# Query and key row transposes issued behind the next projection row block instead of ahead of it

## The chip, the cores and the metric

The kernel runs on one core of a Trainium2 chip. The metric is the device time of one execution in microseconds, of which the median of three runs is given.

## What is computed

One layer of a hybrid decoder for 1024 prompt tokens and 32 sample tokens. One projection `u = RMSNorm(x) @ w_in` gives the columns of three branches (a state-space scan, a dilated attention and a cross-attention), which are merged by gates. The change lies in the attention branch's part of that projection:

```
qkv = qkv.reshape(b, t, ATT_N_GROUPS, 3, ATT_HEADS, ATT_HEAD_DIM)
q = _rope(qkv[:, :, :, 0], pos)
k = _rope(qkv[:, :, :, 1], pos)
v = qkv[:, :, :, 2]
for gi in range(ATT_N_GROUPS):                 # (window, dilation) = (128,1), (512,4), (2048,16)
    o, l = _dilated_prompt(q[:, :, gi], k[:, :, gi], v[:, :, gi], w, d)
```

`_rope` turns the first 16 of each head's 64 columns by an angle that depends on the token. `_dilated_prompt` is a windowed softmax attention in blocks of 128 queries.

## The kernel before

`plan()` writes out one list of steps, `sched`. Every engine walks that list in the same order and issues its own part of each step, so the list fixes the order of work on each engine, and semaphores between engines do the rest. Engines issue in order: an instruction that waits holds back all that stands behind it on its engine.

The attention projection goes by three groups `g` and two halves `h` (four heads, 256 columns each). For each (g, h) there are three chunks of weights, q, k and v, and each chunk has nine row steps `("tok", n, t)`: eight blocks of 128 prompt tokens and one of the sample tokens (t = 8). A row step is on TensorE 24 matmuls of 128x256 (L2287 to L2289, three products of split operands over eight k tiles; for t = 8 of q, k and v 16 matmuls, L2385 and L2386) into one of three PSUM banks. ScalarE evicts it into one of four slots of `rows` (L1515, "eviction" below), VectorE rotates the row there in four instructions (L1820 to L1823, "rotation"; the last one signals `s_rope`). Then the step `("turn", n, t)` transposes the rotated block: two TensorE transposes into bank 3 (L2419), and VectorE copies bank 3 to `QT` or `KT` (L1841, "copy", signals `s_turned`).

`heads_steps` puts these steps in a row. A turn waits in a list, and one is taken out at a row step once three are in it. `around` and `spread` then lay the attention units of the half computed before among the row steps. A unit has the groups: its `scores` (L2441, into banks 3 and 4) with the `ptrans` of the unit before (probabilities transposed, L2458), its `softmax` (no TensorE work), and the `pv` of the unit before (L2483). Each of the five blocks of row steps from (g, h) = (0, 1) to (2, 1) has the eight units 0 to 7 of the half before among its 27 row steps.

Bank 3 is shared by turns and scores, so each waits for the reader of the other:

```
elif s[0] == "turn":                                   # TensorE
    pe.wait_ge(s_rope, roped[("tok", n, t)] + 1)
    if scored_before[s]:
        pe.wait_ge(s_msk3, scored_before[s])           # scores' bank 3 read (DVE L1897)
    if v >= 1:
        pe.wait_ge(s_turned, v)                        # the turn before copied out
elif s[0] == "scores":
    pe.wait_ge(s_turned, max(turns_before[s], ...))    # all turns before it copied out
```

VectorE reads the scores with L1897 ("mask", two instructions; the first signals `s_msk3`). It also makes `w_lo` of coming weights, a step `("low", n)` of one long instruction (L1753). At its end `plan()` puts each of these behind a `pv`, and behind the turn that follows it if one follows directly. Permuting the normalised tokens (`perm`) stands ahead of block (1, 0).

Of the kernel before, what the change touches and what calls it, by code (L numbers as in the profile page):

```python
# [119 lines left out]
def plan():  # L120
# [7 lines left out]
    def chunk(kind, detail, src, col):  # L128
        chunks.append((kind, detail, src, col))
        return len(chunks) - 1  # L130
# [40 lines left out]
    def heads_steps(qkv):  # L171

        steps, waiting = [], []
        for n in qkv:
            kind = chunks[n][0]
            for t in range(NB + 1):
                now = [waiting.pop(0)] if len(waiting) >= 3 or (kind == "v" and waiting) else []
                steps.append(now + [("tok", n, t)])
                if kind != "v" and t < NB:
                    waiting.append(("turn", n, t))  # L180
            steps.append([("split", n)])
        return steps
# [53 lines left out]
    for g in range(NG):  # L236
        for h in range(2):
            qkv = [chunk(k, (g, h), "w_in", C_QKV + g * 3 * AW + j * AW + CW * h) for j, k in enumerate("qkv")]
            if h == 0 and g in PASS_AT:
                sched.insert(len(sched) - 1, ("perm", PASS_AT[g]))  # L240
            sched += around(todo, heads_steps(qkv))
            todo = [unit("att", g, b, h) for b in range(NB)]
# [20 lines left out]
    def gate_steps(k):  # L263

        steps = []
        for n in take(k):
            for s in project(n) + [("split", n)]:
                if s[0] in ("split", "silu"):
                    steps[-1].append(s)
                else:  # L270
                    steps.append([s])
        return steps
# [16 lines left out]
    steps = gate_steps(round(total))  # L289
# [6 lines left out]
    steps = gate_steps(1) + [[]]  # L296
# [22 lines left out]
    steps = []  # L319
    for i in range(4):  # L320
        n = chunk("p1", 2 * i, "att+mem", CW * i)
# [9 lines left out]
    for i in range(4):  # L331
        n = chunk("p2", 2 * i, "w_br_ssd", CW * i)
        sched += [("p2", n, f, j) for f in range(2) for j in range(3)] + [("split", n)]
    for i in range(4):
        n = chunk("out", i, "w_out", CW * i)
# [2445 lines left out]
```

## Time and profile before

| | us |
|---|---|
| median of three runs (lowest, highest) | 2127.19 (2124.83, 2128.45) |
| the profiled execution, its own time | 2122.49 |
| its span in the trace | 2120.6 |
| TensorE matmul busy | 1978.7 (93%) |
| VectorE busy | 984.6 (46%) |
| ScalarE busy | 763.9 (36%) |
| GpSimd busy | 241.5 (11%) |

The profile is of one execution. Its time is the number against which a sum of durations is made; the median of the three runs is what a comparison is made with. The busy share of TensorE counts its matmuls with modelled ends, so what a step costs there is read from the starts of matmuls.

### The profile page before, as it was taken

The page shows a single profiled execution, that of the slowest core. Times are in us where ns is not written, and L with a number is a line of the kernel's source. Part 1 is how long each engine was busy: PE and PEld are TensorE (multiplying, and loading weights), DVE is VectorE, ACT ScalarE, POOL GpSimd, SP SyncE. Part 2 cuts the span into 40 slices and gives each one's busy share as a digit, 9 for nine tenths or more (in the row PEclk, how much of TensorE's full clock was granted, in tenths as well). Part 3 has the DMA queues.
Part 4 walks back from the last instruction along what each step waited for, and adds up shares of the span by engine and source line. Part 5 has one row for each costly group of instructions (what it writes and reads, how often), then busy time and mean ns, then how long its engine had stood idle before and what let it go on. Part 6 is the DMA issues. An engine that isn't in the chain of part 4 may idle for free.

```text
span 2120.6 us, 34809 instructions
## 1 busy us (share of the span) xinstructions
PE 1978.7 (93%) x14301; PEld 1887.0 (89%) x14301; DVE 984.6 (46%) x1941; ACT 763.9 (36%) x1642; POOL 241.5 (11%) x358
## 2 busy tenths in 40 slices
PE   5999999999979999999999899999999859969997
PEld 5899999999979999999999898769999759969997
DVE  5313676535465353534236676103454545454423
ACT  5223354223343333323555322215566532132202
POOL 1001111100001010111111200001121111100000
PEclk9999999999999999999999999999999869989999
DMA  6211332311101111122246675683455536454422
GB/s 216 90 42 52 93 92 82 93 46 48 40 30 51 54 49 57 61 64 83 68 147 220 224 255 163 228 281 124 150 160 176 202 102 191 166 181 137 144 83 105
DMA packets 171742, 257.18 MB, mean 121 GB/s; under 512 B 20229, under 2 KB 115269, under 8 KB 171557
## 3 DMA queue, kind: packets, MB, share of 16 engines
q1 hardware_dynamic: 149328, 187.97, 28.1%
q0 software_dynamic: 22256, 66.98, 9.3%
q8 instruction: 114, 1.87, 0.4%
q14 instruction: 44, 0.36, 0.1%
HBM read 188.13 MB, written 66.76 MB: 120 GB/s over the span
## 4 chain that ended last, share of the span: by engine, by line
PE 76%; DVE 8%; ACT 6%; DMA 5%; issue 3%; SPq 0%; DVEq 0%; POOL 0%; ACTq 0%; POOLq 0%
PE bank L2287 19%; PE bank L2288 19%; PE bank L2289 19%; PE bank L2483 2%; DVE w_lo L1753 2%; PE bank L2698 2%; PE bank L2458 2%; DMA acc<-acc_T 2%; PE bank L2441 1%; PE bank L2587 1%; PE bank L2419 1%; ACT soft L1579 1%; PE bank L2742 1%; PE bank L2520 1%; DMA sums<-sum_T 1%
## 5 line engine op out<-in xcount | busy, mean ns | idle before, releaser
L2287 PE MATMUL bank<-w_hi,hT_hi 128*128 128x256 f32 (+1 forms) x1848 | 535.7, 290 | 1.4 <-issue 1.4
L2288 PE MATMUL bank<-w_lo,hT_hi 128*128 128x256 f32 (+1 forms) x1848 | 523.8, 283 | 0.0
L2289 PE MATMUL bank<-w_hi,hT_lo 128*128 128x256 f32 (+1 forms) x1848 | 522.9, 283 | 0.0
L2287 PE MATMUL bank<-hT_hi,w_hi 128*128 128x352 f32 x1344 | 450.8, 335 | 6.3 <-DVE acc L2134 5.6
L2289 PE MATMUL bank<-hT_hi,w_lo 128*128 128x352 f32 x1344 | 438.9, 327 | 0.0
L2288 PE MATMUL bank<-hT_lo,w_hi 128*128 128x352 f32 x1344 | 438.2, 326 | 0.0
L2287 PEld LDWEIGHTS bank<-w_hi,hT_hi 128*128 128x128 f32 (+1 forms) x1848 | 348.7, 189 | 3.2 <-issue 1.6
L2289 PEld LDWEIGHTS bank<-w_hi,hT_lo 128*128 128x128 f32 (+1 forms) x1848 | 349.6, 189 | 0.6
L2288 PEld LDWEIGHTS bank<-w_lo,hT_hi 128*128 128x128 f32 (+1 forms) x1848 | 348.7, 189 | 1.3
L2287 PEld LDWEIGHTS bank<-hT_hi,w_hi 128*128 128x128 f32 x1344 | 257.7, 192 | 20.1 <-issue 8.4
L2288 PEld LDWEIGHTS bank<-hT_lo,w_hi 128*128 128x128 f32 x1344 | 258.5, 192 | 0.5
L2289 PEld LDWEIGHTS bank<-hT_hi,w_lo 128*128 128x128 f32 x1344 | 256.7, 191 | 0.0
L1753 DVE TENSOR_TENSOR w_lo<-w_raw,w_hi 128x2048 fp32r<-128x2048 f32 x64 | 146.4, 2287 | 199.6 <-ACT w_hi L1425 199.5
L1515 ACT ACTIVATE rows<-bank 128x256 f32<-128x256 f32 (+2 forms) x172 | 65.2, 379 | 329.5 <-PE bank L2289 285.5
L1425 ACT ACTIVATE w_hi<-w_raw 128x2048 fp32r<-128x2048 f32 x64 | 122.1, 1908 | 77.6 <-PE bank L2289 48.9
L1579 ACT ACTIVATE soft<-soft,nmax 128x256 f32<-128x256 f32 (+1 forms) x224 | 100.0, 448 | 80.2 <-DVE nmax L1917 79.9
L1549 ACT ACTIVATE fstage<-bank 128x256 f32<-128x256 f32 (+5 forms) x168 | 56.5, 459 | 142.6 <-PE bank L2289 142.4
L1820 DVE TENSOR_TENSOR small<-rows,con 128x32 f32<-128x32 f32 (+1 forms) x108 | 20.5, 190 | 187.6 <-ACT rows L1515 187.3
L1897 DVE TENSOR_TENSOR soft<-bank,con 128x256 f32<-128x256 f32 (+1 forms) x96 | 47.7, 537 | 51.3 <-PE bank L2441 51.2
L2483 PE MATMUL bank<-V,softT 128*128 128x64 f32 x560 | 67.7, 270 | 0.8 <-issue 0.8
L2483 PEld LDWEIGHTS bank<-V,softT 128*128 128x128 f32 x560 | 66.6, 192 | 1.0 <-issue 1.0
L1946 DVE COPY obuf<-bank 128x256 f32<-128x256 f32 x48 | 20.2, 421 | 99.3 <-PE bank L2483 99.3
(423 smaller groups left out, 2926.1 us busy)
## 6 DMA issues: line engine op xcount, KB each, us to landing
w_raw<-in_w_in SPq DMA_DIRECT2D x96, 512.0 KB, 5.0
kvring<-in_cache_win_kv SPq DMA_DIRECT2D x98, 256.0 KB, 4.7
feat_T<-fstage POOLq DMA_DIRECT2D x40, 528.0 KB, 4.0
fstage<-feat_T SPq DMA_DIRECT2D x16, 528.0 KB, 4.6
xc<-feat_T SPq DMA_DIRECT2D x8, 1024.0 KB, 5.8
sums<-sum_T SPq DMA_DIRECT2D x32, 256.0 KB, 4.5
o_rows<-obuf POOLq DMA_DIRECT2D x48, 132.0 KB, 2.0
mo<-o_rows SPq DMA_DIRECT2D x24, 264.0 KB, 3.6
```

The costliest lines, as they stand in the source:

```text
L1425: act.activation(w_hi[:, n % 2, :, :], w_raw[:, :, :], ACT.Copy).then_inc(s_whi, 1)
L1515: act.activation(dst, psum, func).then_inc(s_pjev, 1)
L1549: ins = act.activation(dst[:, to], psum[:, c0:c1], func)
L1579: ins = act.activation(soft[:, a % 2, h, 0:w], soft[:, a % 2, h, 0:w], ACT.Exp, bias=nmax[:, a % 2, h:h + 1], scale=scale, accum_out=total)
L1753: dve.tensor_tensor(w_lo[:, n % 2, :, :], w_raw[:, :, :], w_hi[:, n % 2, :, :].bitcast(F32), ALU.subtract).then_inc(s_wlo, 1)
L1897: ins = dve.tensor_tensor(dst, src, con[:, c0:c0 + w].unsqueeze(1).broadcast_to([P, 2, w]), ALU.add)
L2287: pe.matmul(out, xh(k), wh(k), start=(k == 0), stop=False)
L2288: pe.matmul(out, xh(k), wl(k), start=False, stop=False)
L2289: ins = pe.matmul(out, xl(k), wh(k), start=False, stop=(k == nk - 1))
L2458: ins = pe.transpose(bank[5 + h // 2][:, c0:c0 + P], soft[:, a % 2, h, P * k:P * k + P], ident)
L2483: ins = pe.matmul(bank[7][:, HD * h:HD * h + HD], softT[:, a % 2, h, k, :], V[:, b0 + k, c0:c0 + HD], start=(k == 0), stop=(k == kb - 1))
L2698: ins = pe.matmul(bank[5 if h < 8 else 7][0:m, SP * (h % 8):SP * (h % 8) + SP], Lm_of(c, h // 4)[:, h % 4, :], xdt[0:m, SP * h:SP * h + SP ...
```

## The change

```diff
@@ heads_steps
             for t in range(NB + 1):
                 now = [waiting.pop(0)] if len(waiting) >= 3 or (kind == "v" and waiting) else []
-                steps.append(now + [("tok", n, t)])
+                steps.append([("tok", n, t)] + now)
                 if kind != "v" and t < NB:
                     waiting.append(("turn", n, t))
```

Which turn is taken out at which row step stays as it was; it now stands behind that row step. So when it is issued, one more row has been projected. In the 96 places where a turn stood ahead of a row step the two swap. `spread` cuts its groups at the ends of row steps, so a turn that is now the last of its row step can stand directly ahead of the next group. No instruction is added or taken away, apart from where VectorE's `w_lo` stands: that step now comes directly behind its `pv` and no longer behind a turn.

**TensorE, block (0, 1), around the scores of unit 5.** Row-step matmuls are L2287 to L2289. Before:

```order
L2289 MATMUL bank<-w_hi,hT_lo 128x256
L2441 MATMUL bank<-KT,QT 128x256 x4
L2458 MATMUL bank<-con,soft 128x128 x8
L2419 MATMUL bank<-con,rows 128x128 x2
L2287 MATMUL bank<-w_hi,hT_hi 128x256
```

Now:

```order
L2289 MATMUL bank<-w_hi,hT_lo 128x256
L2419 MATMUL bank<-con,rows 128x128 x2
L2441 MATMUL bank<-KT,QT 128x256 x4
L2458 MATMUL bank<-con,soft 128x128 x8
L2287 MATMUL bank<-w_hi,hT_hi 128x256
```

The turn behind scores and transposed probabilities went behind the next row step, and another turn came in between the row step and the scores.

**VectorE at the same place**, from the rotation of the row ahead of the scores to the next row's. Before:

```order
L1820 TENSOR_TENSOR small<-rows,con 128x4x8
L1821 TENSOR_TENSOR small<-rows,con 128x4x8
L1822 TENSOR_TENSOR rows<-rows,con 128x4x16
L1823 TENSOR_TENSOR rows<-rows,small 128x4x16
L1897 TENSOR_TENSOR soft<-bank,con 128x2x256 x2
L1929 COPY softT<-bank 128x512
L1841 COPY KT<-bank 128x2x128
L1820 TENSOR_TENSOR small<-rows,con 128x4x8
```

Now:

```order
L1820 TENSOR_TENSOR small<-rows,con 128x4x8
L1821 TENSOR_TENSOR small<-rows,con 128x4x8
L1822 TENSOR_TENSOR rows<-rows,con 128x4x16
L1823 TENSOR_TENSOR rows<-rows,small 128x4x16
L1841 COPY KT<-bank 128x2x128
L1897 TENSOR_TENSOR soft<-bank,con 128x2x256 x2
L1929 COPY softT<-bank 128x512
L1820 TENSOR_TENSOR small<-rows,con 128x4x8
```

The copy of the turn ahead of the scores now stands directly behind the rotation of the newest row, and ahead of the mask.

**VectorE in block (0, 1), ahead of the scores of unit 2**, where `w_lo` (L1753) is made. Before:

```order
L1823 TENSOR_TENSOR rows<-rows,small 128x4x16
L1946 COPY obuf<-bank 128x256
L1841 COPY QT<-bank 128x2x128
L1753 TENSOR_TENSOR w_lo<-w_raw,w_hi 128x2048
L1820 TENSOR_TENSOR small<-rows,con 128x4x8
L1821 TENSOR_TENSOR small<-rows,con 128x4x8
L1822 TENSOR_TENSOR rows<-rows,con 128x4x16
L1823 TENSOR_TENSOR rows<-rows,small 128x4x16
L1897 TENSOR_TENSOR soft<-bank,con 128x2x256 x2
```

Now:

```order
L1823 TENSOR_TENSOR rows<-rows,small 128x4x16
L1841 COPY QT<-bank 128x2x128
L1946 COPY obuf<-bank 128x256
L1753 TENSOR_TENSOR w_lo<-w_raw,w_hi 128x2048
L1820 TENSOR_TENSOR small<-rows,con 128x4x8
L1821 TENSOR_TENSOR small<-rows,con 128x4x8
L1822 TENSOR_TENSOR rows<-rows,con 128x4x16
L1823 TENSOR_TENSOR rows<-rows,small 128x4x16
L1841 COPY QT<-bank 128x2x128
L1897 TENSOR_TENSOR soft<-bank,con 128x2x256 x2
```

The long instruction stays where it was against the output copy (L1946) and the rotation; a copy came in behind that rotation. ScalarE, GpSimd and the DMA queue of SyncE have the same instructions in the same order as before.

## Rows read from the trace of the kernel before

**Rows 1.** The page: TensorE's busy time, and its granted clock in 40 slices.
```profile
PE 1978.7 (93%) x14301; PEld 1887.0 (89%) x14301; DVE 984.6 (46%) x1941; ACT 763.9 (36%) x1642; POOL 241.5 (11%) x358
...
PEclk9999999999999999999999999999999869989999
```
**Rows 2.** Busy time by engine, sum of the five blocks' stretches (432 us).
```profile
sum 432.00, PE 414.01 PEld 394.25 DVE 225.64 ACT 136.95 POOL 41.40; mean PE 82.80 PEld 78.85 DVE 45.13 ACT 27.39 POOL 8.28
```
**Rows 3.** Waits of TensorE, 484 to 1000 us: total, times, longest.
```profile
PE bank L2419 <- DVE rows L1823: 12.1, 12, 2.0
```
**Rows 4.** TensorE in order of time (start, us, line), scores of unit 5.
```profile
538.71 0.28 PE L2289 MATMUL bank<-w_hi,hT_lo 128*128 128x256 f32 x1
538.92 1.13 PE L2441 MATMUL bank<-KT,QT 64*128 64x256 f32 x8
539.98 1.09 PE L2458 MATMUL bank<-con,soft 128*128 128x128 f32 x8
...
541.20 0.36 PE L2287 MATMUL bank<-w_hi,hT_hi 128*128 128x256 f32 x1
```
**Rows 5.** ScalarE and VectorE at the same place.
```profile
539.11 0.38 ACT L1515 ACTIVATE rows<-bank 128x256 f32<-128x256 f32 x1 [2.96 <-PE bank L2289]
...
540.11 0.22 DVE L1823 TENSOR_TENSOR rows<-rows,small 128x64 f32<-128x64 f32 x1
```
**Rows 6.** TensorE, unit 3 of the same block, where no turn follows.
```profile
512.45 0.28 PE L2386 MATMUL bank<-w_lo,hT_hi 128*64 128x256 f32 x1
...
514.56 0.36 PE L2287 MATMUL bank<-w_hi,hT_hi 128*128 128x256 f32 x1
```
**Rows 7.** TensorE and VectorE, unit 6 of block (1, 1).
```profile
781.38 0.28 PE L2386 MATMUL bank<-w_lo,hT_hi 128*64 128x256 f32 x1
782.40 0.72 PE L2441 MATMUL bank<-KT,QT 64*128 64x128 f32 x8 [0.74 <-DVE KT L1841]
...
784.11 0.36 PE L2287 MATMUL bank<-w_hi,hT_hi 128*128 128x256 f32 x1
...
781.84 0.41 DVE L1841 COPY KT<-bank 128x256 f32<-128x256 f32 x1
```
**Rows 8.** TensorE and VectorE, unit 2 of block (0, 1), behind `w_lo`.
```profile
499.14 0.28 PE L2289 MATMUL bank<-w_hi,hT_lo 128*128 128x256 f32 x1
...
502.77 0.36 PE L2287 MATMUL bank<-w_hi,hT_hi 128*128 128x256 f32 x1
...
501.68 0.22 DVE L1823 TENSOR_TENSOR rows<-rows,small 128x64 f32<-128x64 f32 x1
```
**Rows 9.** TensorE, unit 1 of block (1, 0), behind the permutation.
```profile
607.46 0.66 PE L2458 MATMUL bank<-con,soft 128*128 128x128 f32 x4 [2.11 <-ACT soft L1579]
610.13 0.66 PE L2419 MATMUL bank<-con,rows 128*128 128x128 f32 x2 [2.01 <-DVE rows L1823]
...
615.48 0.28 PE L2289 MATMUL bank<-w_hi,hT_lo 128*128 128x256 f32 x1
```
**Rows 10.** TensorE, unit 5 of block (2, 1), one key block per unit.
```profile
978.84 0.28 PE L2289 MATMUL bank<-w_hi,hT_lo 128*128 128x256 f32 x1
979.05 0.72 PE L2441 MATMUL bank<-KT,QT 64*128 64x128 f32 x8
...
981.07 0.37 PE L2287 MATMUL bank<-w_hi,hT_hi 128*128 128x256 f32 x1
```
**Rows 11.** TensorE, unit 1 of block (0, 1).
```profile
486.88 0.27 PE L2289 MATMUL bank<-w_hi,hT_lo 128*128 128x256 f32 x1
...
489.34 0.36 PE L2287 MATMUL bank<-w_hi,hT_hi 128*128 128x256 f32 x1
```
**Rows 12.** By stretch: busy us (count) of PE, PEld, DVE, ACT, POOL; granted clock; DMA.
```profile
608.60:615.40 6.80, 5.27 (x25) 5.30 (x26) 2.63 (x8) 0.00 (x0) 0.00 (x0) 0.50 0.01 4
615.50:1209.30 593.80, 574.13 (x4756) 553.66 (x4755) 278.43 (x728) 232.23 (x598) 84.97 (x154) 1.00 0.29 95
...
1272.60:1275.10 2.50, 0.04 (x1) 0.00 (x1) 2.50 (x3) 0.00 (x0) 0.00 (x0) 0.82 0.40 149
```

## The prediction

> **What bounds the kernel now.** I read the page first, then the five blocks alone, then the waits, then single places in order of time. TensorE is busy for 93% of the span at nearly full clock [rows 1], and for 414.0 of 432 us in the blocks that the change touches, with VectorE at 225.6 and ScalarE at 137.0 [rows 2]. So a microsecond by which TensorE starts its next row step later is a microsecond of the end, and work of the other engines is free unless TensorE waits for it. The waits show what the edit aims at: 12.1 us, 12 times, in which a turn waited for VectorE's rotation [rows 3]. The name is that of an instruction; the semaphore that was late is the mask's, which stands right behind the rotation.
>
> I measure each place by one number: from the start of the last row-step matmul ahead of the scores (T) to the start of the first matmul of the next row step. At unit 5 of block (0, 1) it is 541.20 - 538.71 = 2.49 us [rows 4]; at unit 3, where no turn follows the scores, 514.56 - 512.45 = 2.11 us [rows 6]. The difference, 0.38 us, is what the turn and its wait cost there.
>
> **What the change does at these places.** Each of the five blocks has eight units. Units 0 and 7 have no turn near. Unit 1 loses a turn behind its scores and gets none ahead. Unit 3 gets one ahead of its scores and had none behind. Units 2, 4, 5 and 6 have both: the one behind goes, another comes ahead. The remaining turns only swap with a row step or a `pv` and cost the same there. So 25 scores get a turn directly ahead (5 x 5), and 25 turns behind scores go (units 1, 2, 4, 5, 6).
>
> **The wait that comes.** Scores wait until every turn before them is copied out of bank 3. That copy now stands on VectorE behind the rotation of the newest row, and the rotation waits for the eviction of the very row step that TensorE has just finished. All of it is visible: with T = 538.71 the eviction starts at T + 0.40 and takes 0.38, and the rotation ends at 540.11 + 0.22, T + 1.62 [rows 5]. The copy takes 0.41 us and starts about 0.08 before the rotation's end, as neighbours on VectorE do here, so it ends at T + 1.95. Scores that waited for such a copy exist already: it ended at 781.84 + 0.41 = 782.25, the scores began at 782.40, 0.15 later [rows 7]. New start of the scores: T + 2.09, against T + 0.21 now [rows 4]. Each new wait costs **1.88 us**, the turn's own issue in it included. Nothing hides it, since scores, probabilities and the next row step stand behind it on TensorE.
>
> Nineteen of the 25 are of this kind: 19 x 1.88 = 35.7. In three of them (unit 4 of blocks (0, 1), (1, 0) and (2, 1)) the row is also evicted into a slot whose turn now stands behind it; I add 0.25 us each, about one transpose: 0.7.
>
> In the other six (unit 2 of the first four blocks, unit 4 of the third and fourth) the rotation stands behind `w_lo`. There it ends at 501.68 + 0.22 = 501.90, T + 2.76 [rows 8]. The edit takes a copy of 0.41 from ahead of `w_lo`, but puts one ahead of the previous row maximum, so the exponentials, the eviction behind them, the rotation and the output copy come 0.33 later: net 0.08 earlier. Scores start at T + 2.68 + 0.47 = T + 3.15, which is 2.94 later than now: 6 x 2.94 = 17.6. Together the new waits come to **54.0 us**.
>
> **The waits that go.** A turn behind the scores waited for the mask; now a whole row step is between, so it is covered.
> - Units 4, 5, 6 of the first two blocks: 0.38 at the place shown, 0.64 at unit 4. I take 0.45 x 6 = 2.7.
> - Units 5 and 6 of the next two: at 781.38 the place takes 2.73 [rows 7], of which 1.02 is a wait that stays as part of the new one, and scores and probabilities take the rest but for the turn. A place of this width without a turn, scores at T + 0.21, would take 1.70. So 1.03, at unit 5 about 0.8: 0.92 x 4 = 3.7.
> - Units 2, 4, 5, 6 of the last block: 981.07 - 978.84 = 2.23 [rows 10], and 1.27 without the turn. 0.96, a little more beside `w_lo`: 1.03 x 4 = 4.1.
> - The six behind `w_lo`: 502.77 - 499.14 = 3.63 [rows 8] against 2.11, so 1.52, and 1.65 at the four places of the narrower blocks: 2 x 1.52 + 4 x 1.65 = 9.6.
> - Unit 1: 489.34 - 486.88 = 2.46 [rows 11] against 1.68 (narrow probabilities), 0.78 three times, 0.95 in the last block: 3.3.
> - Unit 1 behind the permutation. The turn begins 2.67 us after the probabilities, and the row step behind it runs at half clock until 615.48 [rows 9, 12]. With the row step directly behind the probabilities it starts at about 607.9 and, if the half clock up to there is as now and ends one step of its length earlier, ends at about 612.2 instead of 615.5. I take 3.3.
>
> Removed in all: **26.7 us**. Everything outside the 40 places costs what it did: block (0, 0) has no units, and its turns and row steps swap freely; `w_lo` comes no later; no DMA moves, and their queues keep their order. What follows the blocks starts later by the same amount and waits for nothing new.
>
> **The sum.** 54.0 - 26.7 = +27.3 us on the profiled execution's 2122.5: 2149.8. The median of the runs lies 4.7 above that execution, so I expect 2127.2 + 27.3 = 2154.5 us, rounded up to **2155**. A new wait cannot be below 0.81 us, the one that exists at 781.38 (1.02 - 0.21), and I see none above the 2.94 behind `w_lo`. With these ends for all 25 the sum is 20.3 - 26.7 = -6.4 and 73.5 - 26.7 = +46.8. I stay with the middle because the chain behind it is in the rows link by link.
>
> **Rivals.**
> *The clock falls.* In the six places behind `w_lo` TensorE would stand idle for about 2.6 us between the turn and the scores, and about 1.5 us in the others. The granted clock was 1.00, its 2.4 GHz level, from 615.5 to 1209.3 us, and 0.50, 1.2 GHz, for 6.8 us from 608.6, around the waits of 2.1 and 2.0 us [rows 9]; it began to fall in a wait of 2.5 us at 1272.6 [rows 12]. A row step at half clock took 5.0 us (610.44 to 615.48) against 2.85. If each of the six places cost one such step, that is 6 x 2.2 = 13 us more: 2168. If all 25 did, 2210, but dense row steps stand on both sides of every wait, and eleven of the twelve waits of [rows 3] lie where the clock stayed at 1.00. The Trainium skill, "TensorE: Matmul & The Clock Gate", section "A second HAM failure mode", says that frequent short idle times between groups of matmuls make the throttle come and go, with a warm-up to pay each time. By that rule the trace agrees only for the stretch at 605 to 615.
>
> *The new wait is short, and the kernel is faster.* If VectorE had the copy done before the rotation of the new row, as at 781.84, where the copy belongs to an earlier turn, each new wait would be 0.81 us and the time 2127.2 - 6.4 = 2121. It decides at 26.7 / 25 = 1.07 us per new wait. Against it: the order on VectorE puts rotation ahead of copy at all 25 places, and the rotation alone ends 1.62 us behind T.
>
> *The waits only trade places.* If both kinds were alike, 25 go and 25 come, and nothing is measured: 2127. The mask's wait is hidden in part by the scores and probabilities (1.9 us of TensorE work), the copy's by nothing, which is why I give it little.
>
> **How the numbers follow.** Forecast 0.74, clock 0.19, shorter wait 0.04, trade 0.03. About 0.2% (4.3 us) is what a measurement of this kernel can tell from no change. The range goes from 2146 (each wait 0.35 us shorter) to 2167 (the clock case for nearly all of the six). Faster 0.04, same 0.03, slower 0.93.
>
> **What would show it.** In the changed kernel's profile: scores (L2441) waiting for VectorE's copies (L1841) about 25 times, some 1.5 us each and 2.6 in six, together near 45 us; the turn's waits (L2419) nearly gone; the places of 2.49 and 2.11 us both at about 4.0; the permutation's place shorter by about 3. It would be wrong if scores begin less than 1.5 us behind T, if turns still wait, or if the granted clock is below 1.00 in the blocks from 620 us on.

## The result and the profile after

| | before | changed |
|---|---|---|
| median of the runs, us | 2126.38 (4 runs, 2124.83 to 2128.45) | 2167.94 (4 runs, 2163.98 to 2170.81) |
| ratio to before, 95% interval | | 1.020 (1.0184 to 1.0216) |
| profiled execution, us | 2122.49 | 2163.98 |
| its span | 2120.6 | 2162.2 |
| from the first to the last attention scores matmul | 598.9 | 643.8 |

The change costs 41.6 us. The forecast was 27.3 (2155, range to 2167): the sign and the new waits held, the size did not, and the result lies just outside the range.

TensorE's waits between 484 and 1060 us in the changed kernel, by what was waited for: us in total, times, longest.

```profile
PE bank L2441 <- DVE QT L1841: 33.7, 15, 3.1
PE bank L2441 <- DVE KT L1841: 14.6, 10, 1.6
PE bank L2313 <- ACT hT_hi L1562: 4.5, 3, 3.3
PE bank L2458 <- ACT soft L1579: 2.1, 1, 2.1
PE bank L2419 <- DVE KT L1841: 1.5, 2, 0.8
```

The scores (L2441) wait for the copy of a turn 25 times, 48.3 us together; the 12.1 us of turns that waited for a rotation [rows 3] are gone. The forecast said 25 times and about 45 us.

The place of [rows 4] and [rows 5], scores of unit 5 in block (0, 1), in the changed kernel. TensorE, ScalarE, VectorE in order of time:

```profile
544.44 0.28 PE L2289 MATMUL bank<-w_hi,hT_lo 128*128 128x256 f32 x1
544.56 0.38 PE L2419 MATMUL bank<-con,rows 128*128 128x128 f32 x2
546.55 1.13 PE L2441 MATMUL bank<-KT,QT 64*128 64x256 f32 x8 [1.61 <-DVE KT L1841]
```
```profile
544.84 0.38 ACT L1515 ACTIVATE rows<-bank 128x256 f32<-128x256 f32 x1 [2.69 <-PE bank L2289]
```
```profile
545.26 0.19 DVE L1820 TENSOR_TENSOR small<-rows,con 128x32 f32<-128x32 f32 x1 [1.59 <-ACT rows L1515]
...
545.84 0.23 DVE L1823 TENSOR_TENSOR rows<-rows,small 128x64 f32<-128x64 f32 x1
545.99 0.42 DVE L1841 COPY KT<-bank 128x256 f32<-128x256 f32 x1
```

With T = 544.44, the start of the last row-step matmul, the eviction begins at T + 0.40, the rotation ends at T + 1.63, the copy at T + 1.97, the scores begin at T + 2.11. The prediction had T + 0.40, 1.62, 1.95 and 2.09.

At unit 2 of block (1, 1), behind `w_lo`, the same chain is longer, and something else comes with it. TensorE, then VectorE:

```profile
746.46 0.28 PE L2289 MATMUL bank<-w_hi,hT_lo 128*128 128x256 f32 x1
746.58 0.38 PE L2419 MATMUL bank<-con,rows 128*128 128x128 f32 x2
749.99 1.23 PE L2441 MATMUL bank<-KT,QT 64*128 64x128 f32 x8 [3.03 <-DVE QT L1841]
...
753.34 0.41 PE L2289 MATMUL bank<-w_hi,hT_lo 128*128 128x256 f32 x1
753.55 0.41 PE L2287 MATMUL bank<-w_hi,hT_hi 128*128 128x256 f32 x1
```
```profile
745.84 0.41 DVE L1841 COPY QT<-bank 128x256 f32<-128x256 f32 x1
746.18 0.41 DVE L1946 COPY obuf<-bank 128x256 f32<-128x256 f32 x1
746.51 2.28 DVE L1753 TENSOR_TENSOR w_lo<-w_raw,w_hi 128x2048 fp32r<-128x2048 f32 x1
748.71 0.18 DVE L1820 TENSOR_TENSOR small<-rows,con 128x32 f32<-128x32 f32 x1
...
749.43 0.42 DVE L1841 COPY QT<-bank 128x256 f32<-128x256 f32 x1
```

The wait is 3.03 us, and the row step behind it issues a matmul every 0.21 us instead of every 0.12. Busy times by stretch (PE, PEld, DVE, ACT, POOL, then the granted clock) show seven such stretches outside the permutation's:

```profile
629.80:636.40 6.60, 6.08 (x27) 5.34 (x28) 2.36 (x5) 0.60 (x1) 0.00 (x0) 0.50 0.52 161
530.80:534.10 3.30, 3.30 (x18) 2.65 (x15) 1.70 (x3) 0.41 (x1) 0.00 (x0) 0.50 0.82 285
749.30:756.00 6.70, 6.01 (x31) 5.82 (x32) 1.99 (x5) 0.60 (x1) 0.00 (x0) 0.50 0.51 159
780.00:786.70 6.70, 6.16 (x32) 5.96 (x33) 1.84 (x5) 0.60 (x1) 0.00 (x0) 0.50 0.52 157
810.70:814.00 3.30, 3.30 (x20) 3.08 (x18) 1.45 (x3) 0.60 (x1) 0.00 (x0) 0.50 0.15 43
899.50:902.80 3.30, 3.30 (x18) 3.30 (x17) 0.69 (x1) 0.60 (x1) 0.00 (x0) 0.50 0.66 234
926.80:930.10 3.30, 3.30 (x20) 3.08 (x19) 1.27 (x3) 0.52 (x1) 0.07 (x1) 0.50 0.20 57
```

In all of them the clock is at 1.2 GHz, half its upper level, and TensorE is nearly always busy, so this is work done slowly and no wait. Before the change the clock was 1.00 from 615.5 to 1209.3 us [rows 12]. These 33 us are the candidate for what the sum lacked; the experiments had to tell them from longer waits. Below, a "fall" is the beginning of such a stretch at half clock.

### The profile page after: what moved, and what is told of

Same layout as the page of the kernel before. It is cut to its first block, busy times and chain, and to the rows that moved or that the text cites. A ratio compares the mean times of both kernels' runs of the same rounds, so it can differ in the third digit from the quotient of the medians.

```text
span 2162.2 us, 34809 instructions
## 1 busy us (share of the span) xinstructions
PE 1984.2 (92%) x14301; PEld 1895.2 (88%) x14301; DVE 988.4 (46%) x1941; ACT 765.1 (35%) x1642; POOL 241.4 (11%) x358
## 4 chain that ended last, share of the span: by engine, by line
PE 75%; DVE 9%; ACT 6%; DMA 6%; issue 3%; SPq 0%; DVEq 0%; ACTq 0%; POOL 0%; POOLq 0%
PE bank L2287 18%; PE bank L2288 18%; PE bank L2289 18%; PE bank L2458 2%; PE bank L2483 2%; PE bank L2441 2%; DVE w_lo L1753 2%; DMA acc<-acc_T 2%; PE bank L2698 2%; PE bank L2587 1%; ACT soft L1579 1%; DMA sums<-sum_T 1%; PE bank L2742 1%; PE bank L2520 1%; PE bank L2386 1%
## 5 line engine op out<-in xcount | busy, mean ns | idle before, releaser
L2287 PE MATMUL bank<-w_hi,hT_hi 128*128 128x256 f32 (+1 forms) x1848 | 538.1, 291 | 1.4 <-DVE hT_lo L2157 1.4
L2289 PE MATMUL bank<-w_hi,hT_lo 128*128 128x256 f32 (+1 forms) x1848 | 524.6, 284 | 0.0
L2287 PE MATMUL bank<-hT_hi,w_hi 128*128 128x352 f32 x1344 | 448.7, 334 | 6.2 <-DVE acc L2134 5.6
L2289 PE MATMUL bank<-hT_hi,w_lo 128*128 128x352 f32 x1344 | 437.1, 325 | 0.0
L2287 PEld LDWEIGHTS bank<-w_hi,hT_hi 128*128 128x128 f32 (+1 forms) x1848 | 351.4, 190 | 3.2 <-issue 1.7
L2289 PEld LDWEIGHTS bank<-w_hi,hT_lo 128*128 128x128 f32 (+1 forms) x1848 | 351.8, 190 | 0.6
L2287 PEld LDWEIGHTS bank<-hT_hi,w_hi 128*128 128x128 f32 x1344 | 256.0, 190 | 19.9 <-issue 8.4
L2289 PEld LDWEIGHTS bank<-hT_hi,w_lo 128*128 128x128 f32 x1344 | 255.5, 190 | 0.0
L1753 DVE TENSOR_TENSOR w_lo<-w_raw,w_hi 128x2048 fp32r<-128x2048 f32 x64 | 146.4, 2287 | 197.3 <-ACT w_hi L1425 197.3
L2441 PE MATMUL bank<-KT,QT 64*128 64x128 f32 (+1 forms) x384 | 46.6, 363 | 48.4 <-DVE QT L1841 33.7
L2441 PEld LDWEIGHTS bank<-KT,QT 64*128 64x128 f32 x384 | 32.0, 198 | 57.3 <-issue 54.7
```

The lines of the kernel that those rows point to most:

```text
L1753: dve.tensor_tensor(w_lo[:, n % 2, :, :], w_raw[:, :, :], w_hi[:, n % 2, :, :].bitcast(F32), ALU.subtract).then_inc(s_wlo, 1)
L2287: pe.matmul(out, xh(k), wh(k), start=(k == 0), stop=False)
L2289: ins = pe.matmul(out, xl(k), wh(k), start=False, stop=(k == nk - 1))
L2441: ins = pe.matmul(bank[3 + h % 2][:, CW * (h // 2):CW * (h // 2) + kb * P], QT[r:r + 64, i, P * b:P * b + P], KTt[r:r + 64, i, P * b0:P * ...
```

## The experiments

Nine kernels ran. "Blocks" is the time from the first to the last attention scores matmul of the profiled execution, which leaves out what varies ahead of and behind the blocks. It is 598.9 us before and 643.8 after. Each ratio is to executions of the kernel before that were taken beside the run; their medians are 2125.6 us (e1 to e4), 2125.9 (e5 to e7) and 2124.7 (e8, e9). Line numbers shift with an edit: the scores (L2441) are L2445 in e1 and e3, L2448 in e2 and L2452 in e5, the turns (L2419) L2423 in e7 and L2426 in e4, the copies (L1841) L1845, L1848 or L1852.

| | what differs | us, median | ratio to before (95%) | blocks, us |
|---|---|---|---|---|
| changed | | 2167.9 | 1.020 (1.0184 to 1.0216) | 643.8 |
| e1 | copy ahead of the rotation | 2130.1 | 1.0028 (1.0014 to 1.0042) | 610.2 |
| e2 | waits filled with transposes | 2161.5 | 1.0167 (1.014 to 1.0195) | 629.8 |
| e3 | `w_lo` behind the scores | 2149.6 | 1.0107 (1.0087 to 1.0128) | 621.5 |
| e4 | turn ahead of the row step before scores | 2168.5 | 1.0199 (1.018 to 1.0218) | 646.1 |
| e5 | e4 and e1 | 2104.6 | 0.990 (0.9883 to 0.9916) | 579.1 |
| e6 | e1 and e3 | 2118.3 | 0.997 (0.9959 to 0.9982) | 594.0 |
| e7 | kernel before with `w_lo` behind the scores | 2120.4 | 0.9978 (0.9967 to 0.9988) | 595.3 |
| e8 | filled behind `w_lo` only | 2154.3 | 1.0145 (1.0127 to 1.0162) | 632.2 |
| e9 | filled elsewhere only | 2166.5 | 1.0203 (1.0188 to 1.0218) | 641.8 |

**e1, the copy ahead of the rotation.** Edit of the changed kernel, VectorE alone:

```diff
-            for s in sched:
+            dve_sched = list(sched)
+            for i in range(len(sched) - 1):
+                if sched[i][0] == "tok" and sched[i + 1][0] == "turn" and chunks[sched[i + 1][1]][0] != "mk":
+                    dve_sched[i], dve_sched[i + 1] = sched[i + 1], sched[i]
+            for s in dve_sched:
```

> The changed kernel, but VectorE does the copy of a turn (L1841) ahead of the rotation of the row step that the turn stands behind; TensorE's order is as in the changed kernel. Theory (the new wait is the chain eviction, rotation, copy): scores begin about 1.1 us behind the last row-step matmul instead of 2.0 at 19 places, and about 0.7 us earlier at the six behind w_lo, 23 us in all, and with shorter waits most falls of the clock go too (another 10 to 14): 2131 to 2137 us. Rival (bank 3 or the transposes themselves set the wait): 2163 to 2168 us.

2130.1 us, 38 less than the changed kernel. TensorE's order is untouched, so the place of the copy behind the rotation is what made the new wait. Waits of TensorE (its lines are shifted by 4):

```profile
PE bank L2445 <- DVE QT L1845: 17.5, 15, 1.9
PE bank L2445 <- DVE KT L1845: 6.1, 10, 0.7
```

25 waits again, now 23.6 us instead of 48.3. This is the forecast's rival of the short wait (0.6 to 0.7 us of idle time at most places without `w_lo`). It lands within 5 us of the kernel before, 1 us under what I expected; the rival's own price, 2121, is reached only in e6 (2118.3), where the waits at `w_lo` are short too. The profiled execution was the slowest of e1's ten (2137.3), so its blocks may be longer than usual.

**e2, e8 and e9, the waits filled.** TensorE transposes the identity into the projection bank that the next row step will overwrite, between the turn and the wait of the scores:

```diff
+                        at = sched.index(s)
+                        near = sched[at - 2:at] if sched[at - 1][0] == "split" else sched[at - 1:at]
+                        if near[0][0] == "turn":
+                            x = proj_before[s]
+                            bank_free(x)
+                            for i in range(24 if any(y[0] == "low" for y in sched[at - 4:at]) else 10):
+                                pe.transpose(bank[x % 3][:, 0:P], ident, ident)
                         pe.wait_ge(s_turned, max(turns_before[s], 2 + (2 * g + half + 1) * 2 * NB))
```

> The changed kernel with transposes of the identity into the free projection bank between each turn and the scores that wait for its copy (10 at most places, 24 behind w_lo); they fit into TensorE's idle time, and their results are overwritten. Theory (part of the loss is TensorE's clock, which fell to half seven times in the blocks): granted clock 1.00 from 640 to 1050 us, scores as late as before, 2151 to 2158 us. Rival (the excess over my sum is longer waits, the clock only shows them): 2166 to 2170 us.

Here more work makes the blocks shorter. The place of unit 5 in e2:

```profile
545.40 0.29 PE L2289 MATMUL bank<-w_hi,hT_lo 128*128 128x256 f32 x1
545.52 0.38 PE L2419 MATMUL bank<-con,rows 128*128 128x128 f32 x2
545.74 1.25 PE L2444 MATMUL bank<-con 128*128 128x128 f32 x10
547.42 1.14 PE L2448 MATMUL bank<-KT,QT 64*128 64x256 f32 x8 [0.43 <-DVE KT L1841]
```

The scores begin at T + 2.02, 0.09 earlier than in the changed kernel; for the rest only the idle time is filled. Busy times from 620 to 1050 us, the changed kernel and then e2; the clock is the number behind POOL's:

```profile
620.00:1050.00 430.00, 389.92 (x3191) 376.00 (x3190) 186.09 (x534) 125.23 (x380) 45.70 (x84) 0.96 0.17 53
```
```profile
620.00:1050.00 430.00, 423.18 (x3610) 409.49 (x3609) 187.76 (x538) 128.73 (x393) 48.31 (x89) 1.00 0.17 56
```

The blocks shrink from 643.8 to 629.8 us. With all the waits and the full clock they are 30.9 us longer than before, and the fallen clock is worth the other 14.0. At four places (unit 4 of the first two blocks, units 2 and 4 of the last: scores at T + 3.05 instead of T + 2.5) the 24 transposes were more than the wait held, about 2 us in all, so the split is good to some 2 us.

The changed kernel's own trace gives nearly the same price without e2's waits. For each of the seven stretches, take the way from its scores to the last row-step matmul ahead of the next scores, and set it against the same steps at full clock in e2. The one at unit 4 of block (0, 1) is longer by 1.6 us, that at 749 us by 2.75, and all seven by 14.7 us. The transfers that run there (DMA 0.38 from 746.5 to 756.5 us) are not what slows it: in e2 the same steps have 0.37 (744.5 to 754.5 us) and a clock of 1.00.

The total was less clear: 2161.5 us (2154.1 to 2166.0), between what the two theories said and not clear of the changed kernel's 2164.0 to 2170.8. In the profiled execution the part behind the blocks was 1053.5 us, 12 more than in that of the changed kernel. Whether that is usual for e2 these runs don't tell. The blocks carry the verdict, and e8 shows it in the total.

> e2 with its filling transposes only at the ten places behind w_lo (24 each), none at the other fifteen. If it is the long waits behind w_lo that drop the clock: granted clock 1.00 beyond the permutation but for one or two falls, the stretch of the five blocks 630 to 635 us as in e2 (629.7). If many waits of 1.5 us do it as well: 638 us or more.

Filled at the ten places behind `w_lo` alone: 2154.3 us (2150.8 to 2156.7, clear of the changed kernel), blocks 632.2, clock 1.00 from 620 to 1050 but for one stretch of 3.4 us.

> The reverse of e8: 10 filling transposes at the fifteen places without w_lo, none at the ten behind it. If the long waits drop the clock: four or more falls beyond the permutation, each behind one of the ten, and the five blocks take 638 to 645 us. If the number of waits does it: 630 to 634 us.

Filled at the fifteen others alone: 2166.5 us, blocks 641.8, as slow as unfilled within its interval. Six falls came beyond 620 us and two ahead of the permutation, each at an unfilled wait of 2.0 to 3.0 us at one of the ten; two others of the ten, of 3.1 and 1.95 us, had none. So in this kernel it is the waits behind `w_lo` that drop the clock; the fifteen others, of 0.95 to 1.6 us, brought one fall in e8. That this is a matter of their length alone is not shown: see e4.

**e3, `w_lo` later.** In the changed kernel:

```diff
+        nxt = [k for k in range(at, min(at + 4, len(sched))) if sched[k][0] == "scores" and sched[k - 1][0] == "turn"]
+        if nxt:
+            sched.insert(nxt[0] + 2, ("low", s[1]))
+            continue
         sched.insert(at + (sched[at][0] == "turn" if at < len(sched) else 0), ("low", s[1]))
```

> The changed kernel, but the 10 w_lo steps that stand ahead of a row step, a turn and scores go behind those scores and their transposed probabilities. Theory (w_lo lengthens the wait and these places drop the clock): scores there at 2.05 us behind the row step instead of 3.5 (6 places) and 2.5 (4), 10 us less, and 3 to 5 falls of the clock less (4 to 8 us): 2150 to 2155 us. If the clock does not hang on these places: 2158 us. If w_lo late makes a later wait instead: 2168 us or more.

2149.6 us, 18 less, just under what I expected. Its waits:

```profile
PE bank L2445 <- DVE QT L1845: 24.6, 15, 1.8
PE bank L2445 <- DVE KT L1845: 14.5, 10, 1.6
```

They are 9.2 us less than in the changed kernel, and no wait for a copy is longer than 1.8 us. But the blocks are 22.3 us shorter. The remaining 13 us is clock: outside the permutation's stretch it fell once (3.4 us). This agrees with e2 by another road, without any added work. Ten `w_lo` steps moved here; six of them are those that the prediction counted, the other four had lengthened their waits too (to T + 2.5). With `w_lo` gone from ahead of them the scores begin at T + 2.11 at unit 2 of every block and at T + 2.25 at unit 4.

**e7, the same in the kernel before.**

> The kernel before with only w_lo moved behind the scores and transposed probabilities. Theory (the sum's 9.6 us at six places are w_lo ahead of the mask): the wait of the turn there shrinks from 1.5 to about 0.4 us, 6 to 7 us less: 2118 to 2120 us. If w_lo then delays the copy for the next turn: 2125 us or more.

2120.4 us, 5.5 less than its base of 2125.9 and 0.4 above the range that I gave. The prediction's 9.6 us for the turns behind `w_lo` is confirmed in kind; the waits of a turn for a rotation, 12.1 us [rows 3], fell to

```profile
PE bank L2423 <- DVE rows L1827: 4.7, 6, 2.0
...
PE bank L2423 <- issue: 1.9, 5, 0.4
PE bank L2423 <- DVE QT L1845: 1.5, 4, 0.5
PE bank L2423 <- DVE KT L1845: 1.5, 4, 0.5
```

The rows for the copies L1845 at turns (L2423) are new: `w_lo` now delays a copy for which the next turn waits, eight times, 3.0 us, so part of the second theory holds too.

**e4, only the turn ahead of scores undone.** In `plan()`, after all steps are laid out:

```diff
+    i = 0
+    while i < len(sched):
+        if sched[i][0] == "scores":
+            j = i - 1 - (sched[i - 1][0] == "split")
+            if sched[j][0] == "turn" and sched[j - 1][0] == "tok":
+                sched[j - 1], sched[j] = sched[j], sched[j - 1]
+        i += 1
```

> The changed kernel, but at the 25 places where a row step and a turn stand directly ahead of scores the turn goes ahead of the row step again. Simple theory (only the turn ahead of scores costs): all 54 us of new waits go, 2127 - 27 = 2100 us. My theory (the copy behind the rotation is what is late, whoever waits for it): each such turn now stands behind a pv and the turn before it, whose copy is behind a rotation that ends about 3 us behind its row step, so a wait of 1 to 2 us stands there: 2125 to 2150 us.

2168.5 us: nothing gained, and worse than my range. No scores wait any more, but the turns do, 25 times:

```profile
PE bank L2426 <- DVE QT L1848: 28.2, 15, 2.6
PE bank L2426 <- DVE KT L1848: 16.5, 10, 2.6
```

One place, TensorE and VectorE:

```profile
495.19 0.38 PE L2426 MATMUL bank<-con,rows 128*128 128x128 f32 x2
495.41 1.00 PE L2490 MATMUL bank<-V,softT 128*128 128x64 f32 x8
498.97 0.41 PE L2426 MATMUL bank<-con,rows 128*128 128x128 f32 x2 [2.56 <-DVE QT L1848]
```
```profile
497.68 0.19 DVE L1827 TENSOR_TENSOR small<-rows,con 128x32 f32<-128x32 f32 x1 [2.41 <-ACT rows L1522]
...
498.41 0.41 DVE L1848 COPY QT<-bank 128x256 f32<-128x256 f32 x1
```

The second turn needs the first one's copy, that copy stands behind the rotation, and the rotation behind an eviction that ScalarE does only after a unit's exponentials. So "the turn ahead of the scores" is not the cause; the copy behind the rotation is, whoever needs bank 3 next. The granted clock fell fourteen times in the blocks, and I had put no price on that either: once at the permutation, eight times at the eight waits of 2.4 to 2.6 us, and five times at waits of 1.57 to 1.69 us, of which e4 has thirteen between 1.5 and 1.7. In e3 twenty-three waits of 1.5 to 1.75 us gave one fall. So the length of a wait alone does not decide; what else differs was not tested. In e4 attention matmuls of 64 columns (`pv`) stand ahead of the wait, in e3 a row step.

**e5, both.** The edits of e1 and e4 together.

> The turn goes ahead of the row step where scores stand behind it (as in e4), and VectorE does a turn's copy ahead of the rotation where the turn stands directly behind a row step (as in e1). Theory (every wait here is for a copy or mask that stands behind a rotation or w_lo): no turn and no scores wait in the five blocks any more, the 26.7 us of the kernel before go and nothing takes their place: 2098 to 2104 us, clock 1.00 in the blocks. Rival (two turns about a pv still wait for each other's copy): 2110 to 2130 us.

2104.6 us, 1.0% faster than the kernel before, within what the first theory said save 0.6 us. The waits for turns' copies in the blocks are down to two (last row):

```profile
PE bank L2324 <- ACT hT_hi L1569: 5.7, 4, 3.3
PE bank L2469 <- ACT soft L1586: 2.1, 1, 2.1
PE bank L2452 <- DVE KT L1852: 1.2, 2, 0.7
```

**e6, e1 with `w_lo` late.** The edits of e1 and e3 together.

> e1 with w_lo behind the scores as in e3. Theory: its six long waits of about 1.9 us become 0.75, 7 us less, and the three or four falls of the clock that e1 has in the blocks beyond the permutation's go, 5 to 6 us less: 2117 to 2120 us. If the clock falls for the number of waits and not for their length, it stays as in e1: 2123 us.

2118.3 us, as expected. Its 25 waits are at most 0.7 us long, and the clock stayed at 1.00 beyond 620 us. In e1 it fell four times outside the permutation's stretch, each time behind one of the waits of 1.75 to 1.9 us at `w_lo`.

## Why the prediction was wrong

- *Which work bounds*: right. Every wait of TensorE in the blocks showed in the time.
- *25 new waits, 25 gone, and which*: right, by the count and the lines of the waits.
- *The chain of a new wait, 1.88 us each*: right within 0.02 us where VectorE is free. Two places missed: unit 6 of the third and fourth blocks, where the scores began at T + 2.38, because the turn itself waited for a copy (the row "L2419 <- DVE KT", 1.5 us in two waits).
- *The slot term, 0.25 us*: wrong in what it held. Scores began at T + 2.45 to T + 2.54 at those units, up to 0.45 behind the plain place. A `w_lo` stands ahead of the rotation there too, which this term left out, and also at unit 2 of the last block (T + 2.51). In e3, without it, unit 4 began at T + 2.25, because the eviction began at T + 0.54 instead of 0.40: the slot is worth 0.14 us, `w_lo` the rest.
- *Behind `w_lo`, T + 3.15*: undersized, and this is the largest error in the waits. I took a copy away from ahead of `w_lo`; but the turn ahead of the `pv` brings another one there. The rows at 745.84 to 746.51 show it: copy, output copy, `w_lo`, where before it was output copy, copy, `w_lo`. The order lists in the section on the change had it already. What stays is the delay of the exponentials by a copy. The scores began at T + 3.49 on average, 0.34 later than forecast, six times: 2.0 us.
- Together the new waits, turns included, came to 57.6 us, not 54.0.
- *The waits that go*: right in kind. e5 has neither these nor the new ones, and its blocks are 19.8 us shorter than before. Of the 26.7 us, 1.2 are the two waits that stayed there, and 5.2 went to the 25 turns, which are issued between other steps then (0.21 each: from unit 1's place to unit 2's it is 10.03 us instead of 9.80); that leaves 20.3. The place behind the permutation gave more than the 3.3 us in the changed kernel: transposed probabilities and row step took 8.0 us before [rows 9] and 3.2 now, at full clock.
- *The clock*: this is the step that failed by most. I made it a rival with a chance of 0.19 and a price of 13 us. The sum put the clock at nothing, and the sign that I had named for it came: 0.96 granted from 620 to 1050 us. The falls cost 14.0 us by e2, 13 by e3 and 14.7 by the changed kernel's own stretches. I argued that dense row steps on both sides of a wait would hold the clock, from eleven short waits (1.3 us at most) and one stretch without falls. No row showed what a wait of 2.6 to 3 us between row steps does. The nearest rows are the waits of 2.1 and 2.0 us at 605 to 610 us and that of 2.5 us at 1272.6, and both places had a fall beside them; they should have weighed more. They do not settle it alone: a wait of 2.2 us that ended at 1149.5 us in the kernel before had no fall.
- *The clock rival's number, 2168*: met by luck in part. It had one fall at each of the six places. There were seven, four of them at those six, and of its other terms the waits were 3.6 us more, the time outside the blocks 3.3 us less.

The account of the blocks: +27.3 as summed, 3.6 more in waits, 14.0 in the clock, 44.9 in all. That it closes to a tenth is chance, since e2's split is good to some 2 us. With 57.6 for the new waits and 14.7 for the clock, 27.4 would be what the old ones gave back. Ahead of and behind the blocks the two profiled executions differ by 3.3 us the other way, so the span grew by 41.6.

What stays open: why the time behind the blocks varies between single profiles (1040.4 to 1047.5 us, and 1053.5 in e2), whether e2 pays there for what it gains, and why one wait is followed by a fall and another of the same length is not.

## What to carry to other kernels

Moving an instruction behind long work hides what it waits for, but whatever then waits for it stands closer: for each move, follow the consumer's whole chain through the in-order engines, and look at the copy or eviction as much as at the instruction. Here the matching order on VectorE, copy before rotation, was worth 38 us, and moving the turn only where it doesn't face the scores another 25. Price idle time of TensorE by its length and, apart from it, by what the clock may do behind it. In the changed kernel the six waits of 2.9 to 3.1 us (17.9 us together) brought four falls, 9.9 us on top. The longest should go first, but e4 shows that waits of 1.6 us are not safe everywhere.

## What the runs showed of the chip that I had not expected

- The granted clock fell at single waits with dense matmuls on both sides: outside the permutation's stretch at waits of 2.0 to 3.1 us in the changed kernel and in e9, at 1.75 to 1.9 us in e1, and five times at about 1.6 us in e4. It was no sure thing: in the changed kernel two of the six waits of 2.9 to 3.1 us (at 501.5 and 870.0 us) had no fall. Two more falls there stood behind waits of 0.95 us at unit 6, where the turn had waited 0.7 to 0.8 us just before. Twenty-five waits of 0.95 to 1.75 us in e3 gave one fall. The Trainium skill, "TensorE: Matmul & The Clock Gate", section "A second HAM failure mode: psum-queue depth-cycling", names frequent micro-idles between groups of matmuls as a cause of falls. The trace agrees that such idle times bring falls, but their number alone does not: e6 has 25 waits of 0.7 us at most and no fall beyond 620 us.
- Work without use in those waits made the kernel faster: 390 transposes whose results are thrown away took 14 us off the blocks (e2), and 240 in the right ten places took 11.6 off (e8), which brought the ratio from 1.020 to 1.0145.
